# Two weight units held in SBUF for the whole program, in the place of two of ten gather buffers

## What is computed

```
z = h @ w_in
gq, gk, gv, gr, glr, dq, dk, dv, gates = split(z)
...
kd = rope(rmsnorm(dk, k_gain), pos);  v_rows = dv
...
x = x + gt1 * mix
...
idx = e1 * PEER_NKEYS + e2
g = softmax(sc)
act = gelu(einsum('td,thkd->thk', xt, peer_u[idx]))
y = einsum('thk,thkd->td', g * act, peer_v[idx])
```

## Time and profile before

| | |
|---|---|
| median of 3 runs | 4398.13 us (4391.16 to 4400.11) |
| the profiled execution | 4400.05 us, its span 4398.3 us |
| busy PE, DVE, ACT, POOL | 3115.6, 2683.3, 1505.7, 1238.0 us |
| moved by DMA | 1518.58 MB, mean 345 GB/s |
| of it by gathers | 1107.36 MB |
| weight loads | 284 of 1024 KB, median 8.3 us from issue to landing |

### The profile page before, as it was taken

The page is one execution under the profiler, slowest core; times in us unless marked ns, Lnnn a source line. Parts: engine busy times, 40 slices in busy tenths (PEclk is TensorE's granted clock), DMA queues, the critical chain, the costliest instruction groups (busy, mean ns, idle before and its releaser), DMA issues.

```text
span 4398.3 us, 48713 instructions
## 1 busy us (share of the span) xinstructions
PE 3115.6 (71%) x15864; PEld 1986.6 (45%) x15864; DVE 2683.3 (61%) x7531; ACT 1505.7 (34%) x3079; POOL 1238.0 (28%) x1068
## 2 busy tenths in 40 slices
PE   6887697897788579768786698866776776433333
PEld 4676574775555247445553365533433464100000
DVE  1324447235767883556777864567679845686775
ACT  3523266223256540222555621134446501010010
POOL 0000111111233332322332322323334323345453
PEclk8798788898888789779886799877777797655555
DMA  7485665688999899999898899999999999999997
GB/s 255 161 318 189 217 233 217 245 328 328 341 355 378 321 363 384 407 364 388 325 384 337 330 392 396 408 351 363 363 367 394 400 412 416 413 400 415 414 412 324
DMA packets 280741, 1518.58 MB, mean 345 GB/s; under 512 B 46329, under 2 KB 91481, under 8 KB 107785
## 3 DMA queue, kind: packets, MB, share of 16 engines
q0 software_dynamic: 152064, 1107.36, 63.0%
q1 hardware_dynamic: 128424, 408.11, 24.9%
HBM read 1474.23 MB, written 40.01 MB: 344 GB/s over the span
## 4 chain that ended last, share of the span: by engine, by line
PE 23%; DMA 21%; DVE 14%; issue 6%; ACT 4%; SPq 1%; POOL 1%; DVEq 0%; ACTq 0%; POOLq 0%
DMA rt_ring<-in_peer_uv,rt_few_idx 12%; PE rt_acc L891 5%; DVE rt_ring L1663 5%; PE pair L639 5%; PE pair L628 4%; DMA dense<-scratch_mod 3%; DMA scratch_scores<-dense 3%; PE bank L639 2%; PE pair L799 2%; PE bank L628 2%; DMA scratch_vh<-dense 2%; DVE rt_diag L1674 1%; DVE negmax L1510 1%; POOL rt_ring L1717 1%; ACT dense L1153 1%
## 5 line engine op out<-in xcount | busy, mean ns | idle before, releaser
L1717 POOL DMA_INDIRECT rt_ring<-in_peer_uv,rt_few_idx x1056 | 1234.7, 1169 | 3126.3 <-PE rt_acc L891 2475.5
L1663 DVE SCALAR_TENSOR_TENSOR rt_ring<-rt_ring,rt_h 128x1024 f32<-128x1024 f32 x1056 | 1260.6, 1219 | 370.6 <-DMA rt_ring<-in_peer_uv,rt_few_idx 355.0
L891 PE MATMUL rt_acc<-rt_ring,rt_diag 128*32 128x512 f32 x4224 | 767.4, 802 | 626.6 <-DVE rt_diag L1674 626.6
L639 PE MATMUL pair<-dense,w 128*128 128x256 f32 (+2 forms) x3056 | 589.9, 351 | 5.0 <-DMA w<-in_weights 3.2
L628 PE MATMUL pair<-w,dense 128*128 128x256 f32 (+1 forms) x2352 | 559.0, 396 | 7.9 <-DMA w<-in_weights 2.0
L639 PEld LDWEIGHTS pair<-dense,w 128*128 128x128 f32 x3056 | 511.1, 196 | 115.8 <-issue 61.3
L891 PEld LDWEIGHTS rt_acc<-rt_ring,rt_diag 128*32 128x32 f32 x4224 | 100.1, 122 | 966.6 <-DVE rt_diag L1674 842.4
L1214 ACT ACTIVATE rt_act_dot<-rt_dot 128x2 f32<-128x2 f32 x528 | 106.2, 202 | 1249.7 <-DVE rt_ring L1663 1247.9
L628 PEld LDWEIGHTS pair<-w,dense 128*128 128x128 f32 (+1 forms) x2352 | 438.6, 190 | 159.5 <-issue 69.7
L1674 DVE TENSOR_SCALAR rt_diag<-cst,rt_act_dot,rt_few_prob 128x32 f32<-128x32 f32 x1056 | 265.5, 295 | 158.3 <-ACT rt_act_dot L1214 153.0
L639 PE MATMUL bank<-dense,w 128*128 128x256 f32 (+2 forms) x1424 | 276.2, 350 | 13.8 <-DMA w<-in_weights 13.8
(11 more groups left out here) (241 smaller groups left out, 3234.5 us busy)
## 6 DMA issues: line engine op xcount, KB each, us to landing
w<-in_weights SPq DMA_DIRECT2D x284, 1024.0 KB, 8.3
rt_ring<-in_peer_uv,rt_few_idx POOLq DMA_INDIRECT x1056, 12.0
dense<-scratch_mod SPq DMA_DIRECT2D x22, 512.0 KB, 14.7
dense<-in_x_prompt SPq DMA_DIRECT2D x16, 512.0 KB, 9.0
scratch_scores<-dense SPq DMA_DIRECT2D x64, 128.0 KB, 8.2
rt_sc<-scratch_scores SPq DMA_DIRECT2D x8, 1024.0 KB, 7.7
rt_h<-scratch_h SPq DMA_DIRECT2D x33, 128.0 KB
rt_x<-scratch_x SPq DMA_DIRECT2D x132, 32.0 KB, 7.1
```

The source lines that it names most:

```text
L639: mm = nc.tensor.matmul(bank[b][:, 0:n], wt[:, k * CH + j * P:k * CH + (j + 1) * P], src[:, k, 0:n], start=(k == 0), stop=(k == KC - 1))
L891: mm = nc.tensor.matmul(acc[u % 2][a * T:(a + 1) * T, :], diag[b % 2][:, i, :], slot[:, D + c * BANK:D + (c + 1) * BANK], start=(q == 0), ...
L1663: dt = nc.vector.scalar_tensor_tensor(up, up, 1.0, h2[u % 2][:], ALU.mult, ALU.mult, accum_out=dot[:, b % 2, i:i + 1])
L1717: nc.gpsimd.indirect_dma_start(ring[n % RING][:], None, d["peer_uv"], bass.IndirectOffsetOnAxis(ap=few_idx[u % 2][:, c:c + 1], axis=0)).th ...
```

## The change

The first unit of the key and of the value projection get SBUF buffers of their own, `kept0` and `kept1`, 8 KB a partition each. They are loaded once, early in SP's list. Both names are taken out of `WEIGHTS`, so all five groups read them from there, and the three `w` buffers go round over a list that is ten entries shorter. The ring has eight places, 64 KB a partition, where it had ten. The views on the ring's last three places move down with it.

```
-B, RING = 2, 10
+B, RING = 2, 8
...
-WEIGHTS = [(g,) + name for g in range(NG) for name in weight_order(g)]
+KEPT = (("dk", 0), ("dv", 0))
+WEIGHTS = [(g,) + name for g in range(NG) for name in weight_order(g) if name not in KEPT]
...
+        kept = [sb(f"kept{i}", [P, KC * CH]) for i in range(len(KEPT))]
...
+        kept_in = [sem(f"kept_in{i}") for i in range(len(KEPT))]
...
             def weights(name):
+                if name[1:] in KEPT:
+                    i = KEPT.index(name[1:])
+                    pe.wait_ge(kept_in[i], 16)
+                    return kept[i]
...
             for t in GROUPS[0][:2]:
                 load_x(t)
+            for i, name in enumerate(KEPT):
+                sp.dma_start(kept[i][:], d["weights"][HPOS[name]]).then_inc(kept_in[i], 16)
             sp.wait_ge(filled, FILLS)
...
                 for name in finished(item):
-                    if WPOS[name] + NW < len(WEIGHTS):
+                    if name in WPOS and WPOS[name] + NW < len(WEIGHTS):
```

## The result

| | median us | lowest to highest | ratio to before, 95% interval |
|---|---|---|---|
| before | 4399.12 | 4391.16 to 4405.0 (4 runs) | |
| changed | 4443.41 | 4440.93 to 4446.18 (4 runs) | 1.0102 (1.0085 to 1.012) |

The change makes the kernel 44 us slower. The profiled execution of the changed kernel has a span of 4444.4 us, 46.1 more than before.

The account below looks back on a forecast made before the run. The prediction took bytes moved by DMA to bound the last 1000 us and nearly the 2400 before. It summed 4400.05 + 62 (ring) - 15 - 5 (loads) + 3 (start) = 4445, less 1.9: 4443 us, range 4375 to 4525.

Parts of the forecast that it names:

- The bound: Bytes bind the last 1000 us and nearly the 2400 us before, which leave the DMA engines some 170 us idle.
- The tail, 0 us: At the end, three-batch turns of 15.6 us with a DMA piece of about 10 keep 2.6 us a gather.
- The cover: In the tail, 5 us between the 10.4 a gather has to land and the shortest landing, 5.4, hides the shorter run-ahead.
- The ring, 62 us: From 1000 to 3600 us, two gathers less in store cost 62 us, between bounds of 26 and 184.
- 12 falls, each at 5.2 us: From 1000 to 3600 us, DMA share falls ending in a full stretch each lack two gathers of 2.6 us.
- The upper bound: Every 20 us stretch with DMA share below 0.9 counts as a fall: 35 in all, 184 us.
- The loads, 15 + 5 us: Groups 2 to 4: six fewer loads save 15 us; group 3's dv steps: earlier weights save a 5.0 us PE wait.
- The start, 3 us: Two kept loads at about 5 us, ahead of biases and the fourth unit, cost 3 us, between 0 and 5.1.
- The forecast of DVE's waits: DVE's total wait for gathers, 355 us before, rises some 40 to 60 us, mostly between 1100 and 3500 us.
- Much slower: Ring was just deep enough, every dip costs: 184 us, 4565 us; sign: DVE waits for gathers in attention; chance 0.14.
- The faster rival: Lane's own transfers land sooner with two fewer gathers ahead: 5.2 us off a 23.7 us store, 77 in all, 4330; chance 0.22.
- The prediction's reading of the page: With DMA engines alternating queues by packet, the number of gathers waiting in the other queue would not matter to a store.

Follow-up runs that it names:

- e4: The changed kernel with six ring places instead of eight: 4978.68 us, ratio 1.1325 to the kernel before.
- e1: The kernel before with eight ring places and nothing else, no kept units: 4443.25 us, ratio 1.0118.
- e5: The kernel before, ten places, but POOL waits as if there were eight in units 0 to 14 (to some 2540 us): 4410.68 us, ratio 1.0029.
- e9: The kernel before, ten places, but POOL waits as if eight in units 18 to 22 (some 2911 to 3468 us): 4417.76 us, ratio 1.0043.
- e10: The kernel before, ten places, but POOL waits as if eight in units 23 to 25 (3468 to 3800 us): 4415.19 us, ratio 1.003.
- e3: The changed kernel with ten places and the two kept units never loaded, their products reading constants instead: 4390.68 us, ratio 0.9981 to the kernel before.
- e14: The kernel before, ten places, but POOL waits as if eight in units 0 to 3 (to some 1250 us): 4393.03 us, ratio 0.9986.

## Why the prediction was right, and which of its terms were not

The forecast was 4443 us and the median is 4443.41, but the sum agrees better than its terms: the ring was priced 10 to 19 us too high, the loads 12 to 20 us too high on the other side, and that the two errors cancel is luck. The direction, and that the loss is made between 1000 and 3800 us and not in the tail, are not.

- **The bound.** Right: the second half is bound by bytes, and the loss shows as DMA share lost there (0.97 to 0.95 from 2540 to 3800 us). One sum is wrong: 170 us of idle DMA time come out with 1.00 as full; with the highest share, 1.02, as the text says, it is 216. No term uses it.
- **The tail, 0 us.** Right, and the turn of three batches with a DMA piece of 10 us is there as described. The tail is 3.5 us longer from unit 26 on. The cover was sized wrongly: the floor of a turn is 13.4 us (e4), so 2.2 us are left of the 5.
- **The ring, 62 us.** The direction and the place in the argument were right, the size was somewhat high: 43 to 52 us (e1). The step that failed is the count: 12 falls, each at 5.2 us. Falls before 2540 us cost 13 us in all (e5), or 19 without the gain of units 0 to 3. What they lack in store can still be fetched, since 7% of the DMA time from 1250 to 2540 us is idle (share 0.93). Falls behind 2540 us cost what was said (e9: +19 for four), and from 3468 us on there are two dips that the count could not have, since it was made on a trace with ten places (e10: +13, of which 5 were in the count). So a low price for the early ones and a surplus late met near the forecast. The upper bound was far too low as a law: with two places fewer again the cost is 535 us, and nothing in the method of counting falls would have said so.
- **The loads, 15 + 5 us.** Oversized: 8 us (e3). The wait of 5.0 us before a product of the dv steps of group 3 is gone. The value stores of that group stay on the chain, with other lengths: 10.55 and 18.86 us where the earlier trace rows has 16.46 and 12.26.

```profile
2013.58 10.55 DMA scratch_vh<-dense
...
2025.00 18.86 DMA scratch_vh<-dense
```

  The step that failed: 2.55 us for each megabyte taken away. It may be right only where the DMA engines have no idle time left; four of the six loads that were priced fall before 2540 us, where 7% of it is idle. But that reason is argued. In e3's trace the part from the first dot product of unit 15 on, where the other two loads are, is no shorter than before (1844 us against 1841), so their 5 us don't show either, and one trace with a spread of a few us can't say where the 8 are gained.
- **The start, 3 us.** 1.75 us by the first product of `dk 0` in the traces.
- **What would show it.** The forecast of DVE's waits failed: it said 40 to 60 us more, and it was 229 more. Waiting of an engine went up five times as much as the time. The reader should not take a rise in waits as a rise in time; the count of dot products by stretch was the better meter.
- **The rivals.** Much slower was refuted for eight places, and is what happens at six. Its sign is there, but small: in the attention of group 4 DVE waits 7.2 us for gathers, where it did not wait, and from the first to the last product of L799 (L806 now) it is 182 us against 177. The faster rival's mechanism exists, with 6 us and not 77 (e14; unit 4 of e5 begins 14 us earlier than before). Its 5.2 us for a store are what was measured (5 us at 491 us), and from 1250 to 2540 us DVE's waits for modulation loads and score stores fall from 51.4 to 28.9 us in the changed kernel and to 29.0 in e5. There it brings nothing: e5 is 13 us slower. That fits the argument against it, that a store that lands sooner does so by gathers that are done later.
  The prediction's reading of the page was wrong. By the rule of the Trainium skill ("DMA: Bandwidth & Descriptors", section on queues, rings and completion order) each DMA engine goes round between its queues packet by packet. The trace agrees (843 packets against 846). But with packets of such different size (6.12 MB against 0.55) the rule does not make the number of waiting gathers indifferent, as the prediction had it; it is why it matters.

The terms by measurement: ring +43 to +52, loads -8 with the start's cost left out, start +2. That gives +37 to +46, and +44 was measured. At eight places e1 is the more direct measure: by the medians all 44 are the ring, and loads and start are 0 together.

## What to carry to other kernels

A prefetch ring's worth is not linear in its places. Compute the shortest turn from a trace in which the ring is too small (here 13.4 us: the fixed part and the landing of the last transfer of a batch, with its sister ahead of it), and compare it with the batches that the ring leaves in flight times the pace; near that point two places are worth 44 us, one step beyond it more than 500. Lost prefetch counts most in stretches where the DMA engines have little idle time left (38 of 51 us here behind 2540 us), so weigh it stretch by stretch; don't count dips of the DMA share on a trace with the larger ring alone, since the smaller one makes new ones; and look at the count of finished work and not at the sum of the waits. Where a short store is waited for and gathers are far ahead, fewer of them in flight let it land sooner.

## What was not expected of the hardware

Two queues with work share the DMA engines by packets and not by bytes: 843 and 846 packets, but 6.12 and 0.55 MB, so that a 128 KB store took 20.4 us behind ten gathers and 15.5 behind eight (e14). The last rows of the line of these stores, 489 to 498 us, in the kernel before and in e14:

```profile
DMA to landing us min/median/max: 18.5/19.5/20.4
```

```profile
DMA to landing us min/median/max: 15.5/15.7/15.8
```

The second gather of a pair needed 7.8 to 8.2 us from its issue to its landing in three turns of e4's tail, with its sister and part of the pair before in the queue, where the shortest landing of any gather before is 5.4 us. And the same waiting can be had at very different prices: 91 us more of DVE's waits for gathers between 1250 and 2540 us moved the work done there by two or three gathers (five or six in e1), 121 us more behind 2540 us by fifteen.
